# Gate and up projection as seven block products, with the second half of the residual scaling on GpSimd released after the block sums

## The chip, the cores and the metric

One Trainium2 chip, one core. The metric is the device time of one execution, in microseconds, as a median of the runs shown. The engines are TensorE (PE: matmuls; PEld: its weight loads), VectorE (DVE), ScalarE (ACT), GpSimd (POOL) and SyncE (SP), which here issues most DMAs. Each engine works through its own queue in order, and semaphores are the only link between queues.

## What is computed

One encoder layer over 1024 tokens of width 1024, in float32: a layer norm, three mixers (a recurrent one, a 2D neighbourhood attention, a latent attention), an output projection with residual and layer norm, then a gated feed-forward part of inner width 2816 with residual and layer norm. What the change touches is the last part:

```python
        mix = jnp.concatenate([o_rw.astype(h.dtype), o_na.astype(h.dtype), o_mla.astype(h.dtype)], -1) @ w_out[l]
        h = layer_norm(DN_ALPHA * h + mix, ln1_g[l], ln1_b[l])
        ff = (jax.nn.silu(h @ w_ffn_gate[l]) * (h @ w_ffn_up[l])) @ w_ffn_down[l]
        h = layer_norm(DN_ALPHA * h + ff, ln2_g[l], ln2_b[l])
```

## The kernel before

The tokens are 8 row tiles of 128 (or two halves of 512 columns, once turned), the width is 8 slices of 128, the inner width FT = 22 column tiles f of 128. A float32 product is made of three products of rounded operands (type float32r): an operand x is split into hi, its rounded copy, made by ScalarE, and lo = x - hi, made by VectorE; the product is hi\*hi + hi\*lo + lo\*hi.

**Output projection and first norm.** `mix_out` (line 2078) forms a row tile in two PSUM banks with plain float32 matmuls (line 2081). VectorE adds the residual (line 1524), takes the statistics (lines 1488 and 1490), and after four tiles normalises them (line 1498). The normalised tiles are turned by `turn1` (line 2098): 8 slices of 4 transposes each (line 2106), the first half ahead of row tile 6, the second after the first part of gate/up. Even slices are scaled and shifted out of PSUM by ScalarE (`copy_even`, line 1029), odd ones by VectorE (`transposed1`, line 1505); ScalarE rounds each (line 1035) and VectorE makes the remainder (line 1509). From the fifth slice on, a transpose waits until its bank is read. The same norm's row-major output is wanted later as the residual: GpSimd scales each row tile in place with two instructions (lines 781 and 783), four tiles after each turn, and SP writes all 4 MB to DRAM (line 621), since the arena has no room for them.

**Gate and up.** `gate_up` (line 2123) makes one tile f: for gate and up (n), two halves (hf), 8 slices (k) and 3 terms, 96 matmuls of 128x128 by 128x512 (line 2130), into four PSUM banks, the four others being used for the next f. SP loads the raw weight tiles (`gate_up_load`, line 612) when the remainder of the tile before is made; ScalarE makes the rounded copy (`weights_hi`, line 1013), VectorE the remainder (`weights_lo`, line 1512), two tiles ahead. Silu of gate is ScalarE's (line 1048), the product with up is VectorE's (line 1542). Four engines run this as a loop of two tiles; the other stages around it are straight code.

**Down.** The product of the activations with w_down is already made as seven block products in the manner of Strassen and Winograd, in four phases: `RING` (line 58) lists the steps of three phases of 11 steps with two products each (w = 0, 1), 24 matmuls of 128x512 per step (line 2152), and the last product runs alone as phase 3, row tile by row tile. ScalarE (`left_hi`, `right_hi`) and VectorE (`left_lo` line 1551, `right_lo` line 1556) split the operands into a ring of four left and two right slots; VectorE makes block sums of the activations (`sums_of_left`, line 1568) and of w_down (`sums_of_right`, line 1581, `last_of_right`, `difference_of_right`). Between phases it adds the finished products to the residual (`add_product`, line 1604), which SP has brought back. After the third phase VectorE takes the statistics of the last norm (`half_stats`, line 1624), and `centre2` and `scale2` finish six row tiles; two others go to ScalarE and GpSimd (POOL_ROWS = 2).

## Time and profile before

| | |
|---|---|
| median of 3 runs | 1831.33 us (1828.92 to 1832.34) |
| profiled execution | 1832.07 us |
| its span, first to last instruction | 1830.3 us |
| busy: TensorE / VectorE / ScalarE / GpSimd | 92% / 51% / 30% / 20% |
| mean granted clock of TensorE | 0.97 |
| moved over HBM | 93.6 MB, mean 51 GB/s |

"Busy" is the share of the span in which an engine executes; matmuls overlap in TensorE's pipeline, so that the mean length of one is more than the distance between two. The stages that matter lie in the span thus: output projection 975 to 1100, gate and up 1100 to 1598, down products 1598 to 1815, last norm to 1830.

### The profile page before, as it was taken

What the parts mean: (1) busy time and instruction counts of PE and PEld (TensorE: products, weight loads), DVE (VectorE), ACT (ScalarE), POOL (GpSimd) and SP (SyncE); (2) the same over time, 40 slices, a digit from 0 to 9 for tenths busy, and PEclk for the clock granted to TensorE, in tenths of its full rate; (3) what the DMA queues carried; (4) which work ended last, traced back from release to release, by engine and by line L of the source; (5) the groups of instructions that cost most, each with busy time, mean ns of one, the idle gap of its engine ahead of it and who ended that gap; (6) DMA issues with size and microseconds to landing.
All of it is one profiled execution on the core that took longest, in us unless ns stands there. A gap on an engine that the chain in (4) does not pass through costs nothing.

```text
span 1830.3 us, 22866 instructions
## 1 busy us (share of the span) xinstructions
PE 1676.0 (92%) x8984; PEld 1225.0 (67%) x8984; DVE 940.0 (51%) x1327; ACT 552.0 (30%) x1028; POOL 359.6 (20%) x363
## 2 busy tenths in 40 slices
PE   2999987868899997899999997999999999999996
PEld 1788755634556654577774445888888888877885
DVE  7314427866675664667665456211111111299878
ACT  3111147733444332444431012111111111133450
POOL 0800001105600000878870044000000000000002
PEclk9999999988999999899999998999999999999998
DMA  5221000000000000000005001211111111164422
GB/s 199 91 93 46 12 30 1 1 16 1 5 9 4 4 0 15 2 3 2 2 2 218 12 12 69 93 55 59 46 46 46 46 46 46 43 199 159 152 70 92
DMA packets 22703, 93.62 MB, mean 51 GB/s; under 512 B 2576, under 2 KB 4944, under 8 KB 20576
## 3 DMA queue, kind: packets, MB, share of 16 engines
q1 hardware_dynamic: 22160, 87.27, 13.5%
q0 software_dynamic: 464, 5.28, 0.7%
q8 instruction: 52, 0.85, 0.2%
q14 instruction: 27, 0.22, 0.0%
HBM read 79.92 MB, written 12.58 MB: 51 GB/s over the span
## 4 chain that ended last, share of the span: by engine, by line
PE 82%; DVE 11%; ACT 3%; issue 2%; DMA 1%; POOL 0%; SPq 0%; ACTq 0%; DVEq 0%; POOLq 0%
PE psum L2130 26%; PE psum L1724 9%; PE psum L2152 8%; PE psum L2081 6%; PE psum L1882 6%; PE psum L1871 4%; PE psum L1742 2%; PE psum L1850 2%; PE psum L1806 2%; PE psum L1824 1%; PE psum L1787 1%; PE psum L1749 1%; PE psum L1980 1%; PE psum L1976 1%; DVE arena L1283 1%
## 5 line engine op out<-in xcount | busy, mean ns | idle before, releaser
L2130 PE MATMUL psum<-h_hi,w_hi 128*128 128x512 f32 x704 | 275.2, 391 | 11.7 <-DVE h_lo L1509 11.7
L2130 PE MATMUL psum<-h_hi,w_lo 128*128 128x512 f32 x704 | 274.6, 390 | 0.0
L2130 PE MATMUL psum<-h_lo,w_hi 128*128 128x512 f32 x704 | 274.6, 390 | 0.0
L1542 DVE TENSOR_TENSOR arena<-psum,arena 128x1024 f32 (+1 forms) x22 | 27.0, 1225 | 391.2 <-ACT arena L1048 391.2
L2130 PEld LDWEIGHTS psum<-h_hi,w_hi 128*128 128x128 f32 x704 | 132.7, 189 | 39.7 <-DVE h_lo L1509 12.0
L2130 PEld LDWEIGHTS psum<-h_lo,w_hi 128*128 128x128 f32 x704 | 132.7, 188 | 27.8 <-issue 0.2
L2130 PEld LDWEIGHTS psum<-h_hi,w_lo 128*128 128x128 f32 x704 | 132.6, 188 | 27.5
L788 POOL TENSOR_TENSOR arena<-arena 128x1024 f32<-128x1024 f32 x2 | 5.8, 2888 | 655.0 <-ACT arena L1102 655.0
L743 POOL TENSOR_TENSOR arena<-arena,consts 128x512 f32<-128x512 f32 x64 | 80.9, 1285 | 232.0 <-ACT arena L984 231.4
L1882 PE MATMUL psum<-arena 128*128 128x512 f32 x256 | 123.8, 608 | 0.0
L1293 DVE TENSOR_REDUCE stats<-psum 128x1 f32<-128x1024 f32 x64 | 78.0, 1224 | 74.6 <-PE psum L1850 74.0
L2081 PE MATMUL psum<-arena 128*128 128x512 f32 x256 | 112.7, 600 | 1.8 <-DMA arena<-in_w_out 1.8
L2152 PE MATMUL psum<-right_hi,left_hi 128*128 128x512 f32 x264 | 103.5, 392 | 5.3 <-DVE right_lo L1559 5.3
L1724 PE MATMUL psum<-h_hi,w_in_hi 128*128 128x512 f32 x240 | 96.7, 403 | 11.1 <-DVEq L1144 11.1
L1048 ACT ACTIVATE arena<-psum 128x1024 f32 (+1 forms) x22 | 22.6, 1027 | 273.4 <-PE psum L2130 273.3
L2152 PE MATMUL psum<-right_hi,left_lo 128*128 128x512 f32 x264 | 103.5, 392 | 0.0
L2152 PE MATMUL psum<-right_lo,left_hi 128*128 128x512 f32 x264 | 103.4, 392 | 0.0
L1724 PE MATMUL psum<-h_lo,w_in_hi 128*128 128x512 f32 x240 | 96.0, 400 | 0.0
L1724 PE MATMUL psum<-h_hi,w_in_lo 128*128 128x512 f32 x240 | 95.1, 396 | 0.0
L945 ACT ACTIVATE arena<-psum 128x1024 f32<-128x1024 f32 x64 | 65.0, 1022 | 91.0 <-PE psum L1871 90.6
L2081 PEld LDWEIGHTS psum<-arena 128*128 128x128 f32 x256 | 48.9, 192 | 64.6 <-issue 60.4
L754 POOL TENSOR_TENSOR arena<-arena,consts 128x512 f32<-128x512 f32 x64 | 79.9, 1269 | 16.7 <-DVE arena L1426 11.6
(286 smaller groups left out, 3118.4 us busy)
## 6 DMA issues: line engine op xcount, KB each, us to landing
arena<-in_w_gate SPq DMA_DIRECT2D x22, 512.0 KB, 3.2
arena<-in_w_up SPq DMA_DIRECT2D x22, 512.0 KB, 4.5
arena<-in_w_down SPq DMA_DIRECT2D x22, 512.0 KB, 3.7
arena<-in_w_down SPq DMA_DIRECT2D x11, 1024.0 KB, 4.8
arena<-in_w_in SPq DMA_DIRECT2D x15, 512.0 KB, 3.6
arena<-in_x SPq DMA_DIRECT2D x8, 512.0 KB, 10.6
resid_spill<-arena POOLq DMA_DIRECT2D x1, 4096.0 KB, 12.9
arena<-in_w_out SPq DMA_DIRECT2D x8, 512.0 KB, 6.4
```

Source lines behind the costliest of these rows:

```text
L743: pool.tensor_tensor(Lev[d][m % 2], Araw[i % 2][d], four_heads(cst((C_LV if d == 0 else C_LVT) + m - 1)), ALU.mult).then_inc(lev_ready, 1)
L754: pool.tensor_tensor(Xt[d].rearrange("p h (k c) -> p h k c", c=32), spread(Xtcs[i % 2][d]), own_block, ALU.mult).then_inc(xt_full, 1)
L945: act.activation(halves(e_ring[kt % NE]), psum[:, 2 * (kt % 2):2 * (kt % 2) + 2, :], ACT.Exp, scale=MLA_SCALE).then_inc(e_ready, 1)
L1293: v.tensor_reduce(g_max[:, b, t:t + 1], psum[:, g_banks, :], AX.XY, ALU.max, negate=True).then_inc(g_max_ready, 1)
L1724: mm = pe.matmul(bank(2 * b + hf), w[:, P * k:P * k + P], x[k][:, cols], start=(k == 0 and n == 0), stop=(k == KT - 1 and n == 2))
L1742: mm = pe.matmul(bank(t), x[k][:, t * P:(t + 1) * P], wv_parts[k // 2][:, HALF * (k % 2):HALF * (k % 2) + HALF], start=(k == 0 and n == 0) ...
L1806: mm = pe.matmul(bank(4 + b, P), na_et[:, b, j * P:(j + 1) * P], vals[:, first // 2 + j, hp * P:(hp + 1) * P], start=(j == 0), stop=(j == 3))
L1871: mm = pe.matmul(bank(2 * (kt % 2) + hf), k_part[b][0:rows, keys_at], q_part[b][0:rows, hf * HALF:(hf + 1) * HALF], start=(n == 0), stop=( ...
L1882: mm = pe.matmul(bank(6 + hf), vh[b][:, kt, :], e_ring[kt % NE][:, hf * HALF:(hf + 1) * HALF], start=(kt == 0), stop=(kt == NT - 1))
L2081: mm = pe.matmul(bank(mixed_bank(t) + hf), mix[:, k, t * P:(t + 1) * P], w_out[k][:, hf * HALF:(hf + 1) * HALF], start=(k == 2), stop=(k = ...
L2130: mm = pe.matmul(bank(4 * b + 2 * n + hf), w[b][n][:, P * k:P * k + P], x[k][:, cols], start=(k == 0 and i == 0), stop=(k == KT - 1 and i ...
L2152: mm = pe.matmul(bank(4 * w + t), x[:, t * P:(t + 1) * P], right_part(p, part), start=(first and n == 0), stop=(last and n == 2), skip_gro ...
```

## The change

Gate and up of one tile become one 2x2 block problem: the weight side has the blocks gate and up, each with its first and its last 512 of the 1024 inner rows; the other side has the same two halves of the width, by two halves of the tokens. Seven block products replace eight. `FF` is the order of the 154 products, written out for each engine; nothing of this stage is a loop any more. A product is 4 slices x 3 terms = 12 matmuls and uses three PSUM banks per tile (x, y, z); a bank is copied by ScalarE, and read again by VectorE, between the products that accumulate in it.

- VectorE makes 8 double-width sums of the turned rows once (`sum5`, `sum6`, `sum7`, `sum4`) with their remainders (`sum_lo`), and four block sums of raw weights per tile (`block_sum`), three adds of PSUM to copies (`add_part`), two multiplications (`times_up`), and every second tile one sum for the down stage (`first_sum`). ScalarE rounds seven weight halves of 128x512 per tile (`part_to_hi`) into a ring of seven slots, copies PSUM three times (`copy_part`) and makes two silus.
- Both engines prepare the first weight halves between the row tiles of the output projection; of this, two block sums and one remainder are placed after row tile 5.
- GpSimd's scaling of row tiles 4 to 7 waits for the last remainder of the turned block sums. SP writes the residual in two halves.
- The activations of the first 12 tiles go to DRAM (`act_spill`), and come back for the first phase of the down product; 10 stay. Two places of tiles lie in `consts`.
- In the down stage the tiles are paired otherwise, one of the four left sums is made ahead, the left sums trail the steps by two, there are three buffers for the wide w_down tiles instead of two, and half of the last statistics are taken earlier.
- The host reorders w_down for the new pairs.

```diff
+FF = [(0, 1), (0, 2), (1, 1), (1, 2)] + [(f, p) for p in (3, 5, 6, 7, 4) for f in range(2)]
+FF += [(2, p) for p in (1, 5, 2, 6, 3, 7)]
+FF += [(f - (p == 4), p) for f in range(3, FT) for p in (1, 4, 5, 2, 6, 3, 7)] + [(FT - 1, 4)]
...
+            for f in range(2, FT):
+                sp.wait_ge(part_lo, FF_AT[f - 2, 7])
+                sp.dma_start(raw_gate[f % 2], a["w_gate"][f]).then_inc(weights_in[f % 2], 16)
+                sp.wait_ge(part_lo, FF_AT[f - 2, 4])
+                sp.dma_start(raw_up[f % 2], a["w_up"][f]).then_inc(weights_in[2 + f % 2], 16)
+                if f == 4:
+                    put_residual(1)
+                if f % 2 == 0 and 0 <= f - 4 < BACK:
+                    if f > 4:
+                        sp.wait_ge(act_out, 16 * (f - 4))
+                    put_out(f - 4)
+                    put_out(f - 3)
...
             for t in range(NT):
                 pool.wait_ge(ln_tr, 2 * KT + 8 * (t // 4 + 1))
+                if t == 4:
+                    pool.wait_ge(h_lo_ready, 2 * KT + OPERAND_AT[4])
                 own.add(pool.tensor_tensor(resid[:, t, :], resid[:, t, :], ln1_rows[0], ALU.mult))
...
```

VectorE's queue from the second turn on (the steady block last):

```diff
+            turned(1, 5)
+            turned(1, 7)
+            for i in range(2):
+                sum5(i)
+            for i in range(2):
+                sum_lo(5, i)
+            for i in range(2):
+                sum6(i)
+            part_to_lo(0, 7)
+            for i in range(2):
+                sum_lo(6, i)
+            for f in range(2):
+                add_part(f, 0)
...
+            part_to_lo(0, 4)
+            for i in range(2):
+                sum_lo(4, i)
+            for f in range(2):
+                add_part(f, 1)
+            part_to_lo(1, 4)
+            own.wait()
+            for f in range(2):
+                add_part(f, 2)
+            block_sum(2, 0)
+            part_to_lo(2, 1)
+            block_sum(2, 1)
+            for f in range(2):
+                times_up(f, 1)
+            part_to_lo(2, 5)
+            part_to_lo(2, 2)
+            block_sum(2, 2)
+            for f in range(2):
+                times_up(f, 0)
+            part_to_lo(2, 6)
+            part_to_lo(2, 3)
+            block_sum(2, 3)
+            part_to_lo(2, 7)
+            first_sum(1)
...
+            for f in range(2, FT):
+                last = f == FT - 1
+                if not last:
+                    block_sum(f + 1, 0)
+                    part_to_lo(f + 1, 1)
+                if f > 2:
+                    times_up(f - 1, 0)
+                part_to_lo(f, 4)
...
+                    block_sum(f + 1, 1)
+                    part_to_lo(f + 1, 5)
+                add_part(f, 0)
...
```

TensorE's product and its waits, and the changed order of additions and left sums between the phases on VectorE:

```diff
+            def ff_product(f, p):
+
+                x, y, z = (4 * (f % 2) + i for i in range(3))
+                if p == 1 and f >= 2:
+                    pe.wait_ge(ff_ready, count_at(2, f - 2, 1))
...
+                elif p == 6:
+                    pe.wait_ge(part_copied, count_at(3, f, 0))
+                elif p == 7:
+                    pe.wait_ge(part_copied, count_at(3, f, 2))
+                elif p == 4:
+                    pe.wait_ge(part_added, count_at(3, f, 2))
+                if f == 0:
+                    pe.wait_ge(h_lo_ready, 2 * KT + OPERAND_AT[p])
...
+                for i, (w, h) in enumerate(((hi, h_hi_p), (hi, h_lo_p), (lo, h_hi_p))):
+                    if i == 2:
+                        pe.wait_ge(part_lo, FF_AT[f, p])
+                    for k in range(4):
+                        mm = pe.matmul(bank({2: z, 3: y, 5: y}.get(p, x)), w[:, P * k:P * k + P],
+                                       h[k // 2][:, HALF * (k % 2):HALF * (k % 2) + HALF],
+                                       start=(fresh and i == 0 and k == 0), stop=(i == 2 and k == 3), skip_group_check=True)
+                mm.then_inc(ff_done, 1)
...
+            sums_of_left(HF - 2)
+            sums_of_right(0)
+            step_lo((1, 0))
+            sums_of_right(1)
             v.wait_ge(resid2_in, 16 * NT)
...
+            for w in range(2):
+                add_products(0, w)
             for f in range(HF):
-                step_lo((1, f))
+                if f:
+                    step_lo((1, f))
                 if f == 0:
-                    add_products(0)
+                    sums_of_left(HF - 1)
                 last_of_right(f)
-                if f + 1 < HF:
-                    sums_of_right(f + 1)
+                if f + 2 < HF:
+                    sums_of_right(f + 2)
```

## Rows read from the trace of the kernel before

**Rows 1.** The page: busy times, the chain by engine and line, costliest group

```profile
PE 1676.0 (92%) x8984; PEld 1225.0 (67%) x8984; DVE 940.0 (51%) x1327; ACT 552.0 (30%) x1028; POOL 359.6 (20%) x363
...
PE 82%; DVE 11%; ACT 3%; issue 2%; DMA 1%; POOL 0%; SPq 0%; ACTq 0%; DVEq 0%; POOLq 0%
PE psum L2130 26%; PE psum L1724 9%; PE psum L2152 8%; PE psum L2081 6%; PE psum L1882 6%; PE psum L1871 4%; PE psum L1742 2%; PE psum L1850 2%; PE psum L1806 2%; PE psum L1824 1%; PE psum L1787 1%; PE psum L1749 1%; PE psum L1980 1%; PE psum L1976 1%; DVE arena L1283 1%
...
L2130 PE MATMUL psum<-h_hi,w_hi 128*128 128x512 f32 x704 | 275.2, 391 | 11.7 <-DVE h_lo L1509 11.7
```

**Rows 2.** Windows: stretch, length, busy by engine (count), granted clock, DMA share, GB/s

```profile
1150.00:1600.00 450.00, 450.00 (x1987) 372.74 (x1986) 71.12 (x63) 68.48 (x71) 0.00 (x0) 1.00 0.14 47
...
984.00:990.00 6.00, 6.00 (x16) 2.65 (x15) 4.49 (x3) 2.11 (x2) 0.00 (x0) 1.00 1.01 437
...
1072.00:1080.00 8.00, 8.00 (x18) 3.52 (x17) 8.00 (x5) 1.73 (x3) 7.84 (x4) 0.89 0.00 0
...
1128.00:1130.00 2.00, 2.00 (x6) 1.52 (x6) 2.00 (x1) 0.00 (x0) 1.92 (x2) 0.50 0.00 0
...
1606.00:1608.00 2.00, 2.00 (x7) 1.58 (x6) 1.97 (x4) 0.00 (x0) 0.00 (x0) 0.56 0.90 209
```

**Rows 3.** The chain in order of time: start, length, what ran

```profile
1110.59 0.45 PE psum L2106 x4
...
1117.31 4.78 DVE h_lo L1509 x2
...
1122.81 4.80 DVE h_lo L1509 x2
...
1127.65 470.06 PE psum L2130 x2064
```

**Rows 4.** TensorE's waits from 900 us on: total, times, longest

```profile
PE psum L2130 <- DVE h_lo L1509: 11.7, 1, 11.7
PE psum L2152 <- DVE right_lo L1559: 5.3, 3, 2.2
PE psum L2106 <- DVE arena L1505: 3.9, 3, 1.6
```

**Rows 5.** Groups from 1000 us on, as in the page's fifth part

```profile
L1554 DVE TENSOR_TENSOR left_lo<-arena,left_hi 128x512 fp32r<-128x512 f32 x66 | 44.5, 688 | 11.8 <-ACT left_hi L1070 11.7
...
L1070 ACT ACTIVATE left_hi<-arena 128x512 fp32r<-128x512 f32 x66 | 41.2, 630 | 82.8 <-PE psum L2152 81.9
...
L1559 DVE TENSOR_TENSOR right_lo<-arena,right_hi 128x1024 fp32r<-128x1024 f32 x33 | 40.4, 1224 | 5.9 <-ACT right_hi L1083 5.9
...
L1048 ACT ACT_TABLE_LOAD x7 | 9.0, 1283 | 128.5 <-PE psum L2130 128.5
```

**Rows 6.** DMA issues from 930 us on: median us from issue to landing

```profile
arena<-in_w_up SPq DMA_DIRECT2D x22, 512.0 KB, 4.5
...
arena<-resid_spill SPq DMA_DIRECT2D x1, 4096.0 KB, 18.2
```

**Rows 7.** Timeline of VectorE and GpSimd in the second turn

```profile
1115.11 1.48 DVE L1509 TENSOR_TENSOR h_lo<-arena,h_hi 128x512 fp32r<-128x512 f32 x2
...
1117.22 4.86 DVE L1509 TENSOR_TENSOR h_lo<-arena,h_hi 128x512 fp32r<-128x512 f32 x2
1122.01 0.80 DVE L1505 TENSOR_SCALAR arena<-psum,par 128x512 f32<-128x512 f32 x1
...
1127.52 6.71 DVE L1514 TENSOR_TENSOR w_lo<-arena,w_hi 128x1024 fp32r<-128x1024 f32 x2
...
1118.87 2.67 POOL L783 TENSOR_TENSOR arena<-arena 128x1024 f32<-128x1024 f32 x1
```

**Rows 8.** Timeline of TensorE: first matmul after each of the two longer stops

```profile
1605.16 0.47 PE L2152 MATMUL psum<-right_hi,left_hi 128*128 128x512 f32 x1 [2.01 <-DVE right_lo L1559]
...
1669.11 0.47 PE L2152 MATMUL psum<-right_hi,left_hi 128*128 128x512 f32 x1 [2.23 <-DVE right_lo L1559]
```

**Rows 9.** Timeline of VectorE in the last norm: one half statistic of sixteen

```profile
1807.41 0.68 DVE L1625 BATCH_NORM_STATS2 stats<-arena 128x6 f32<-128x512 f32 x1
```

More of the change, by code:

```diff
@@ L64, with count_at, first_of @@
 NSLOTS = 4
+TURN_BANKS = (3, 7, 1, 5)
 POOL_ROWS = 2
+FF = [(0, 1), (0, 2), (1, 1), (1, 2)] + [(f, p) for p in (3, 5, 6, 7, 4) for f in range(2)]
+FF += [(2, p) for p in (1, 5, 2, 6, 3, 7)]
+FF += [(f - (p == 4), p) for f in range(3, FT) for p in (1, 4, 5, 2, 6, 3, 7)] + [(FT - 1, 4)]
+FF_AT = {p: n + 1 for n, p in enumerate(FF)}
+NPARTS = 7
+OPERAND_AT = {1: 4, 2: 8, 3: 12, 5: 14, 6: 16, 7: 18, 4: 20}
+KEPT = 10
+BACK = FT - KEPT
+def count_at(each, f, n):
+    return 2 * n + f + 1 if f < 2 else each * f + n + 1
+def first_of(step):
+    return BACK + 2 * step if step < KEPT // 2 else 2 * step - KEPT
 NDR, NDC = 15, 31
@@ L369, in mixed_bank @@
+        h_part = {p: [[rounded(f"h{p}_{part}{i}", 1024 * at[i], 1024) for i in range(2)] for part, at in
+                      zip(("hi", "lo"), H_PLACES[p])] for p in H_PLACES}
+        T_SUMS = {5: b_first[1], 6: b_second[1], 7: b_first[0], 4: b_second[0]}
+        summand = reg(1024 * 43, 1024).rearrange("p (b c) -> p b c", b=2)
         def mixed_bank(t):
             return 0 if t == 2 else 4 + 2 * (t % 2)
-        w_hi = [[rounded(f"w_hi{b}{n}", *tiles(40 + 4 * b + 2 * n, 1)) for n in range(2)] for b in range(2)]
@@ L374, in hybrid_encoder @@
-        w_lo = [[rounded(f"w_lo{b}{n}", *tiles(41 + 4 * b + 2 * n, 1)) for n in range(2)] for b in range(2)]
-        EARLY = 14
-        def act_tile(f):
-            return reg(1024 * (f + 8 if f < EARLY else f - EARLY), 1024)
-        def act_at(f, hf):
-            return 1024 * (f + 8 if f < EARLY else f - EARLY) + HALF * hf
-        def act_half(f, hf):
-            return reg(act_at(f, hf), HALF)
-        wd_one = [reg(1024 * n, 1024) for n in (22, 23)]
-        wd_both = [reg(1024 * n, 2048).rearrange("p (d f c) -> p d f c", d=2, f=2) for n in (38, 22)]
@@ new lines, in silu @@
+            def silu(f, n):
+                act.wait_ge(part_added, count_at(3, f, n))
+                act.activation(act_half(f, n), act_half(f, n), ACT.Silu).then_inc(silu_ready, 1)
+            for f, p in FF[0:4]:
+                part_to_hi(f, p)
+            sd1(0)
+            for f, p in FF[4:7]:
+                part_to_hi(f, p)
+            turned(0, 0)
+            for n in range(KT):
+                turned_hi(0, n)
+                if n % 2 == 0 and n + 2 < KT:
+                    turned(0, n + 2)
@@ L1090, in step_hi @@
                 right_hi(step)
-            silu(act_tile(FT - 2), 0, 0, FT - 2)
-            step_hi(STEPS[0])
-            silu(act_tile(FT - 1), 1, 0, FT - 1)
-            for step in STEPS[1:]:
+            for f in range(2, FT):
+                last = f == FT - 1
+                copy_part(f, 0)
+                if not last:
+                    part_to_hi(f + 1, 1)
+                part_to_hi(f, 4)
+                copy_part(f, 1)
+                if last:
+                    step_hi(STEPS[0])
+                else:
+                    part_to_hi(f + 1, 5)
+                    part_to_hi(f + 1, 2)
+                silu(f, 0)
+                copy_part(f, 2)
+                if last:
+                    step_hi(STEPS[1])
+                else:
+                    part_to_hi(f + 1, 6)
+                    part_to_hi(f + 1, 3)
+                silu(f, 1)
+                if not last:
+                    part_to_hi(f + 1, 7)
+            for step in STEPS[2:]:
                 step_hi(step)
@@ L1532, in _ @@
                     normalise1(hf)
[L1533 to L1549 removed]
+            for f, p in FF[7:10]:
+                part_to_lo(f, p)
```

640 lines of the change are left out of this document (438 added, 202 removed).

## The prediction

> **What bounds the kernel now.** I read the page first: its busy row and its chain. TensorE is busy for 92% of the span and carries 82% of the chain, and the largest line on it is 2130, the gate and up projections [rows 1]. So a change in the number of matmuls there is worth what a matmul costs there. The windows say what that is: 1,987 matmuls in 450 us at a granted clock of 1.00, 0.2265 us from start to start, with VectorE busy for 71 us and ScalarE for 68 [rows 2]. The 390 ns that the page gives for one matmul [rows 1] is its length in the pipeline, not its cost.
>
> The chain in order of time shows where TensorE stops [rows 3]. Between the turn of the second half of the normalised rows at 1110.59 and the 2,064 back-to-back matmuls that begin at 1127.65, only 32 short transposes run, and 4.78 and 4.80 us go to two pairs of small subtractions on VectorE. The waits of TensorE in the last 930 us are few: 11.7 us there, 3.9 us in the first turn, 5.3 us in the down projection [rows 4]. So this stage and all of the down projection except three stops run at TensorE's pace, and the last 15 us are VectorE's alone.
>
> Timings refer to the profiled execution, 1832.07 us with a span of 1830.3; it is 0.7 us above the median of the three runs, 1831.33. The working calls the start of the second turn T, a product one of the seven (12 matmuls, 2.72 us), f a column tile.
>
> **1. The matmuls.** Before, 2 projections x 2 halves x 8 slices x 3 split terms = 96 per tile, 2,112 in all. After, 7 products x 4 x 3 = 84, 1,848 in all. 264 go, at 0.2265: **-59.8 us**. The row includes everything a matmul costs there, and the new ones have the same shape. The Trainium skill, TensorE: Matmul & The Clock Gate, "Wait — 56ns, not 53.3ns?", gives 215.7 ns start to start for 512 columns at the full clock; the row here is 226.5 ns, and by the page the term would be -56.9.
>
> **2. Does the new steady block stay at TensorE's pace?** One tile is 84 matmuls, 19.0 us. VectorE gets 7 weight remainders, 4 block sums, 3 adds from PSUM, 2 multiplications and half a sum for the down stage: 16.5 operations of 128x512 at 0.69 = 11.4 us (the adds out of PSUM I put at the same). ScalarE gets 7 rounded copies, 3 copies from PSUM and 2 silus, 12 at 0.63 = 7.6 us [rows 5]. Neither is a bound. The tight waits are product 7 on the copy taken after product 6, and product 4 on the add taken after product 7: each has one product, 2.72 us, between, and needs one operation of 0.63 or 0.69 and some 0.2 us of signalling. Weight halves are due six products ahead. I cost the waits at nothing; if the cover went it would be about 1 us a wait. An up tile lands in 4.5 us [rows 6] and is issued five products, some 14 us, before its first use; the gate tile earlier: nothing. The spill of 12 tiles, two per two tiles, goes behind the refill on SP, at a stage that moves 47 GB/s [rows 2]: nothing.
>
> **3. The first turn.** VectorE now makes two block sums and one remainder ahead of its first copy of the turn. Before, that copy followed directly on the statistics, and TensorE waited 3.9 us for it and the next [rows 4]. Three operations at 0.6 delay it: +1.9. The longer stop lengthens the low clock behind it: the eight microseconds after the turn show 0.89 [rows 2]. I take +0.8, between 0 and 2. **+2.7 us**.
>
> **4. The second turn and the first two tiles**, the hard part. The four raw quarters are there at T+6.9, by the rows of before (0.8 us a copy, 0.6 a remainder, no GpSimd yet). From there VectorE works through a chain: 8 sums and 8 remainders of 128x1024 at 1.2 us [rows 5], and 7 operations of 128x512 at 0.66, 23.8 us: T+30.7. I add 1 us for a table load of ScalarE (1.28 us, [rows 5]) and handovers: T+31.7. TensorE has ten products in this stretch (27.2 us) and waits in between.
>
> Then GpSimd is released for rows 4 to 7. The timeline shows what that does [rows 7]. A VectorE operation with both inputs in SBUF waits until the running GpSimd instruction ends: two subtractions that take 1.48 us alone took 4.86, and two of double width 6.71, each ending just behind an instruction of GpSimd. Copies from PSUM (0.80) did not wait. The Trainium skill, SBUF — State Buffer, "Who interferes with whom", says that such an instruction and a GpSimd one that reads SBUF exclude each other, whichever came first; the trace agrees, and this speaks against the new place of GpSimd's work, since VectorE has no slack there either.
>
> GpSimd has 8 instructions of about 2.75 us, 22 us, T+53.7. In VectorE's queue behind the last remainder stand eight operations with two SBUF inputs before tile 0's last multiplication: the remainder of (1,4), sum 0 of tile 2, remainder (2,1), sum 1, the two multiplications of half 1, remainders (2,5) and (2,2). One passes for each GpSimd instruction, T+54.3; then a sum and the multiplication out of PSUM, T+55.7. Product (2,1) waits for that multiplication: it starts at T+56. Without GpSimd, it would start about T+41.
>
> Taking out the ten products leaves 28.8 us, against 17.1 before: **+11.7 us**. The restart behind the stop costs the same half clock in both (0.50, that is 1.2 GHz, in the window at 1128, [rows 2]): nothing. Bounds of this term: -3 (no hold by GpSimd) and +20 (a wait at every handover).
>
> **5. Into the down projection.** Before, the sums of the left blocks stood ahead of the first step, TensorE waited 2.01 us [rows 8] and restarted at a clock of 0.56 [rows 2]. After, the last product 4 and the first two steps are split ahead, and the sums come later. The stop goes (2.0), and the low clock (1.8). Next in line is the multiplication for bank 4, with 2.0 us of matmuls in front of it: enough. **-3.8 us**.
>
> **6. First to second phase.** Before, TensorE waited 2.23 us behind eight additions, one last sum of the right side, two sums, and a step [rows 8]. After, one tile's three left sums (1.9 us) are put behind the eight additions too, and steps still can't run further ahead, since ScalarE fills slots as TensorE frees them. The wait grows to about 4.7 and may bring a low clock of 1 us: **+3.5 us**, between 0 and 5. The second change of phase has the same operations in another order: nothing. DMA: 6 MB of spilled tiles come back during a phase of 60 us with 12.5 MB beside them, 310 GB/s against the 437 that the trace reaches at 984 [rows 2]. Nothing, up to 4 us late.
>
> **7. The end.** Eight half statistics leave the stretch behind the down products; four of them come back inside the last additions. Four remain saved, at 0.60 from start to start [rows 9]: **-2.4 us**. The last product is ready before VectorE asks for it in both kernels, so all of it counts.
>
> The sum: -59.8 + 2.7 + 11.7 - 3.8 + 3.5 - 2.4 = **-48.1**, so 1832.1 - 48.1 = **1784 us**.
>
> **Rivals.** *A. GpSimd's rows hold nothing up.* The operations waited for would be of the kind that pass. Product (2,1) starts at T+41: term 4 falls by 15 and the low clock of the restart (2 us) goes: 1767. For it: TensorE has two products of tile 0 and 1 in that time. Against: rows 7, and the queue as counted. 0.14.
>
> *B. Small stops in the steady block.* The one-product covers are thinner than I think, for instance because a remainder ahead of the add on VectorE waits for ScalarE. 0.5 to 1 us in 20 tiles, 10 to 20 us: about 1799. Against: 5 to 7 us of slack on both engines per tile. 0.18.
>
> *C. The up tile comes late* and the result is **slower than before**. SP issues it only after product 4's remainder, one queue in order with spills. It has some 14 us. It would have to land 16.6 us after its issue for the 20 tiles to lose the 48 us (2.4 each); at the 18.2 us that the big reload of 4 MB needed [rows 6], each of 19 tiles loses 4.2, 80 us: 1864. Against: 4.5 us measured, on a nearly empty queue. 0.03.
>
> *D. The release doesn't do what it says*: GpSimd's rows are short of overlap because VectorE's operations get in first, and GpSimd is the one that is delayed. Then its work spreads to T+60 and VectorE's ends near T+48: 1776, inside the range. 0.05.
>
> **Chances.** The forecast as worked out 0.58, A 0.14, B 0.18, C 0.03, D 0.05, anything else 0.02. Range 1766 to 1801: it takes A and B in, with the bounds of terms 3, 4 and 6 around the forecast, and leaves C and the rest out. No change (within 0.2%, about what a measurement of this kernel can tell) would need 45 us of stops: 0.01. Slower 0.03, faster 0.96.
>
> **What would show it.** Right: 1,848 matmuls of this kind; 0.2265 us each and no wait from tile 3 on; a stop of over 10 us ahead of (2,1), released by a VectorE multiplication out of PSUM; during it, VectorE operations with two SBUF inputs of 2 to 3 us beside GpSimd's rows; no stop at the first step of the down projection; one of 4 to 5 us at the second step of the second phase. Wrong: waits that return in every tile (B), waits for gate or up loads (C), or (2,1) at T+41 (A).

## The result and the profile after

| | before | after |
|---|---|---|
| median of 4 runs each, same chip | 1831.07 us (1828.92 to 1832.34) | 1780.11 us (1779.13 to 1782.65) |
| after / before, 95% interval | | 0.9725 [0.9708, 0.9742] |
| profiled execution / span | 1832.07 / 1830.3 us | 1779.13 / 1777.3 us |
| busy: TensorE / VectorE / ScalarE / GpSimd | 92 / 51 / 30 / 20% | 91 / 63 / 36 / 20% |

The medians are 51.0 us apart, the profiled spans 53.0. "Profiled execution" is the one run of each kernel that left a trace. The profiled execution of after is its fastest run, 1.0 us under the median.

The page of after, beside [rows 1] (its last line beside [rows 6]):

```profile
PE 1617.0 (91%) x8720; PEld 1177.7 (66%) x8720; DVE 1115.0 (63%) x1627; ACT 642.3 (36%) x1224; POOL 357.6 (20%) x363
...
PE 80%; DVE 12%; ACT 3%; issue 2%; DMA 1%; POOL 1%; SPq 0%; DVEq 0%; ACTq 0%; POOLq 0%
...
L1746 DVE TENSOR_TENSOR part_lo<-arena,part_hi 128x512 fp32r<-128x512 f32 x154 | 113.2, 739 | 87.1 <-ACT part_hi L1118 87.1
...
arena<-in_w_up SPq DMA_DIRECT2D x22, 512.0 KB, 3.5
```

There are 264 fewer matmuls and 300 more VectorE instructions. The 154 remainders took 739 ns on average, though most take 0.69: a few of them were held, and the timeline will show which. An up tile lands 3.5 us after its issue, against 4.5 in [rows 6].

TensorE's waits from 900 us on (total, times, longest), beside [rows 4]:

```profile
PE psum L2539 <- DVE arena L1799: 11.6, 1, 11.6
PE psum L2556 <- DVE right_lo L1903: 5.7, 2, 4.7
PE psum L2490 <- DVE arena L1696: 4.4, 2, 3.3
PE psum L2539 <- DVE arena L1782: 4.2, 1, 4.2
PE psum L2539 <- DVE arena L1696: 3.2, 1, 3.2
```

Line 2539 is the product's matmul, 1799 the multiplication by up out of PSUM, 1782 the adds out of PSUM, 1903 the right remainder of the down stage. The 11.6 us stand ahead of product (2,1), as forecast. The windows, beside [rows 2] (stretch, length, busy by engine and count, granted clock, DMA share, GB/s):

```profile
1200.00:1540.00 340.00, 340.00 (x1502) 281.53 (x1501) 192.93 (x290) 128.61 (x216) 0.00 (x0) 1.00 0.22 72
...
1614.00:1616.00 2.00, 0.03 (x1) 0.06 (x1) 2.00 (x4) 0.64 (x1) 0.00 (x0) 0.50 0.90 377
1616.00:1618.00 2.00, 2.00 (x5) 1.61 (x6) 1.34 (x3) 0.00 (x0) 0.00 (x0) 0.50 0.49 115
1618.00:1620.00 2.00, 2.00 (x7) 1.52 (x6) 2.00 (x4) 0.00 (x0) 0.00 (x0) 0.50 0.88 348
```

In the steady block a matmul starts every 340 / 1502 = 0.2264 us at a clock of 1.00, as before the change, with VectorE busy for 57% of it. Behind the stop at the second phase of the down products the clock is 0.50, that is 1.2 GHz. The chain in order of time, beside [rows 3] (start, length, what ran; line 2464 is the output projection):

```profile
983.17 77.27 PE psum L2464 x180
...
1069.18 28.41 PE psum L2464 x64
1097.59 10.90 PE psum L2539 x48
...
1163.54 379.75 PE psum L2539 x1668
```

What held the multiplication is seen on VectorE and on GpSimd, beside [rows 7]. VectorE:

```profile
1145.43 2.85 DVE L1746 TENSOR_TENSOR part_lo<-arena,part_hi 128x512 fp32r<-128x512 f32 x1
1148.39 2.69 DVE L1758 TENSOR_TENSOR arena<-arena 128x512 f32<-128x512 f32 x1
1151.00 5.59 DVE L1796 TENSOR_TENSOR arena<-arena 128x512 f32<-128x512 f32 x2
1156.52 5.57 DVE L1746 TENSOR_TENSOR part_lo<-arena,part_hi 128x512 fp32r<-128x512 f32 x2
1162.19 0.69 DVE L1762 TENSOR_TENSOR arena<-arena 128x512 f32<-128x512 f32 x1
1162.80 1.28 DVE L1799 TENSOR_TENSOR arena<-psum,arena 128x512 f32<-128x512 f32 x2
```

GpSimd, the first and the last of its eight instructions:

```profile
1139.85 2.35 POOL L874 TENSOR_TENSOR arena<-arena,consts 128x1024 f32<-128x1024 f32 x1 [49.99 <-DVE h_lo L1738]
...
1158.87 2.67 POOL L876 TENSOR_TENSOR arena<-arena,consts 128x1024 f32<-128x1024 f32 x1
```

While GpSimd runs, operations that need 0.69 us alone take 2.7 to 2.9; the next behind its last instruction (1161.54) takes 0.69 again. T, the start of the second turn, is 1108.48 here (1097.59 + 10.90), so GpSimd starts at T+31.4 and ends at T+53.1, and (2,1) starts at T+55.1. TensorE, its first matmul behind three stops, beside [rows 8]:

```profile
1143.40 2.08 PE L2539 MATMUL psum<-h_hi,part_hi 128*128 128x512 f32 x4 [4.23 <-DVE arena L1782]
1163.54 2.07 PE L2539 MATMUL psum<-h_hi,part_hi 128*128 128x512 f32 x4 [11.60 <-DVE arena L1799]
1615.97 0.77 PE L2556 MATMUL psum<-right_hi,left_hi 128*128 128x512 f32 x1 [4.65 <-DVE right_lo L1903]
```

### The profile page after: what moved, and what is told of

Read it like the earlier page. It is cut to its first block, busy times and chain, and to the rows that moved or that the text cites. A ratio compares the mean times of both kernels' runs of the same rounds, so it can differ in the third digit from the quotient of the medians.

```text
span 1777.3 us, 23088 instructions
## 1 busy us (share of the span) xinstructions
PE 1617.0 (91%) x8720; PEld 1177.7 (66%) x8720; DVE 1115.0 (63%) x1627; ACT 642.3 (36%) x1224; POOL 357.6 (20%) x363
## 4 chain that ended last, share of the span: by engine, by line
PE 80%; DVE 12%; ACT 3%; issue 2%; DMA 1%; POOL 1%; SPq 0%; DVEq 0%; ACTq 0%; POOLq 0%
PE psum L2539 23%; PE psum L2107 9%; PE psum L2556 9%; PE psum L2464 6%; PE psum L2265 6%; PE psum L2254 5%; PE psum L2125 2%; PE psum L2233 2%; PE psum L2189 2%; PE psum L2207 1%; PE psum L2170 1%; PE psum L2132 1%; PE psum L2363 1%; PE psum L2359 1%; DVE arena L1473 1%
## 5 line engine op out<-in xcount | busy, mean ns | idle before, releaser
L2539 PE MATMUL psum<-h_hi,part_hi 128*128 128x512 f32 x616 | 168.4, 396 | 19.1 <-DVE arena L1799 11.6
L1746 DVE TENSOR_TENSOR part_lo<-arena,part_hi 128x512 fp32r<-128x512 f32 x154 | 113.2, 739 | 87.1 <-ACT part_hi L1118 87.1
L2539 PE MATMUL psum<-h_lo,part_hi 128*128 128x512 f32 x616 | 166.9, 393 | 0.0
L2539 PE MATMUL psum<-h_hi,part_lo 128*128 128x512 f32 x616 | 165.6, 391 | 0.0
L1118 ACT ACTIVATE part_hi<-arena 128x512 fp32r<-128x512 f32 x154 | 96.1, 627 | 148.1 <-PE psum L2539 119.3
L2539 PEld LDWEIGHTS psum<-h_hi,part_hi 128*128 128x128 f32 x616 | 117.1, 191 | 45.2 <-DVE arena L1799 12.0
L2539 PEld LDWEIGHTS psum<-h_lo,part_hi 128*128 128x128 f32 x616 | 117.3, 190 | 24.8
L2539 PEld LDWEIGHTS psum<-h_hi,part_lo 128*128 128x128 f32 x616 | 116.4, 189 | 24.4
```

What stands on the lines that cost most here:

```text
L1118: act.activation(part_ring[(FF_AT[f, p] - 1) % NPARTS][0], raw[:, at:at + HALF], ACT.Copy).then_inc(part_hi, 1)
L1746: v.tensor_tensor(lo, raw[:, at:at + HALF], hi, ALU.subtract).then_inc(part_lo, 1)
L2539: mm = pe.matmul(bank({2: z, 3: y, 5: y}.get(p, x)), w[:, P * k:P * k + P], h[k // 2][:, HALF * (k % 2):HALF * (k % 2) + HALF], start=(fre ...
```

## The experiments

All are edits of after, except one of before. Two kinds of number are given. The median is that of unprofiled and profiled runs together. The experiments ran on three chips, each time beside before, whose median there was 1830.4 to 1831.2 us; the ratio is to that before. The stage lengths come from the one profiled execution of each kernel and are taken from T, because the unchanged code ahead took differing times (see the last section). G is where the chain in order of time reaches the down products, the end is the end of the span:

| kernel | T | T to G | G to end | T to end | median, us | ratio [95% interval] |
|---|---|---|---|---|---|---|
| before | 1110.59 | 487.1 | 232.6 | 719.7 | 1831.07 | 1 |
| after | 1108.48 | 434.8 | 234.0 | 668.8 | 1780.11 | 0.9725 [0.9708, 0.9742] |
| pool_old | 1111.53 | 432.8 | 233.5 | 666.3 | 1778.99 | 0.9717 [0.9701, 0.9733] |
| pool_late | 1116.34 | 429.9 | 233.6 | 663.5 | 1779.83 | 0.972 [0.9704, 0.9736] |
| mult_first | 1110.89 | 429.7 | 234.9 | 664.6 | 1777.05 | 0.9704 [0.9688, 0.972] |
| pool_spread | 1112.71 | 419.8 | 234.7 | 654.5 | 1768.87 | 0.9658 [0.9642, 0.9674] |
| no_rows | 1108.02 | 419.0 | 233.5 | 652.5 | 1762.31 (one run) | |
| before_held | 1110.18 | 481.2 | 232.5 | 713.7 | 1824.63 | 0.9963 [0.9948, 0.9979] |
| turn_early | 1107.71 | 436.3 | 233.3 | 669.6 | 1778.02 | 0.971 [0.9694, 0.9726] |
| left_later | 1111.55 | 434.8 | 231.4 | 666.2 | 1779.47 | 0.9722 [0.9705, 0.9738] |
| seven_more | 1111.34 | 434.8 | 234.0 | 668.9 | 1782.61 | 0.9738 [0.9722, 0.9754] |
| three_edits | 1108.75 | 419.8 | 231.7 | 651.5 | 1762.57 | 0.9626 [0.9604, 0.9647] |
| four_edits | 1108.93 | 419.8 | 226.7 | 646.5 | 1757.88 | 0.9602 [0.9582, 0.9622] |

One execution is a weak measure of a small difference. In the seven edits of after that leave its down stage alone, G to end is 233.3 to 234.9 us, and after and seven_more, which stop at the same places, agree to 0.1 us from T on, while turn_early is 1.5 us longer from T to G with the same stops in the second turn. Differences below some 2 us in one of these columns are therefore not read as effects, unless a stop of TensorE in the trace changed by that much.

### Where GpSimd's rows 4 to 7 run

**pool_old**: released by the turn alone, as in before.

```diff
-                if t == 4:
-                    pool.wait_ge(h_lo_ready, 2 * KT + OPERAND_AT[4])
```

> The changed kernel (1780.1 us) without the wait of GpSimd for the last turned remainder: rows 4 to 7 are scaled from about T+5 on, as in the kernel before. My theory (one VectorE operation with two SBUF inputs per GpSimd instruction, wherever the eight instructions stand): eight operations of the turned sums are held instead of eight behind them, 16 us more in the chain up to the last remainder, and 13 us plus 2 us of low clock less after it; product (2,1) starts at T+57 to T+58 instead of T+55.1, 1782 to 1784 us. Rival 1 (in the old place the hold is covered, so the new place only costs): 1767. Rival 2 (the release is a large part of the gain): over 1792.

The hold moved into the turn and the chain of turned sums. Eight operations of VectorE are held there, one per GpSimd instruction, and six of them are double-wide. One of GpSimd's eight instructions:

```profile
1126.47 3.38 POOL L872 TENSOR_TENSOR arena<-arena,consts 128x1024 f32<-128x1024 f32 x1
```

TensorE from its last stop of this stretch on, ahead of product (0,4), to the first matmuls of (2,1):

```profile
1158.88 1.68 PE L2537 MATMUL psum<-h_hi,part_hi 128*128 128x512 f32 x4 [2.96 <-DVE arena L1780]
...
1166.07 1.07 PE L2537 MATMUL psum<-h_hi,part_hi 128*128 128x512 f32 x4
```

(0,4) began at T+47.4 instead of the T+34.9 of after, but (2,1) stood right behind the pair, at T+54.5, without a stop of its own: GpSimd was done, and the multiplications were worked off in the shadow of (0,4) and (1,4). That is 3 us before the T+57 to T+58 expected, and the median of 1779.0 lies below the 1782 to 1784 expected. The last turned remainder came 13.7 us later than in after (T+44.9 against T+31.2), not 16: held operations fell together with waits for ScalarE that VectorE has there anyway (1.5 and 0.3 us in after). Behind it 14.2 us were saved, not 13. T to end is 2.5 us shorter than in after: (2,1) comes 0.5 earlier, its 1,668 matmuls take 378.2 us instead of 379.75, since they don't begin at half clock (at 0.2264 each they would take 377.6), and 0.5 lies behind G, where nothing was changed. So on the median the new release condition gains nothing by itself, against the old one.

**pool_late**: released two tiles later, with the last weight remainder of tile 2.

```diff
                 if t == 4:
-                    pool.wait_ge(h_lo_ready, 2 * KT + OPERAND_AT[4])
+                    pool.wait_ge(part_lo, FF_AT[2, 7])
```

> The changed kernel with rows 4 to 7 released only after the last weight remainder of tile 2 (product 7). My theory: product (2,1) starts at about T+42 instead of T+55.1 and without the long low clock, 14.5 us less there; but in the 22 us of GpSimd's work VectorE passes 8 operations with two SBUF inputs where the steady block wants 14, so that the adds out of PSUM queued behind them come late and TensorE stops in tiles 3 and 4, 5 to 10 us in all: 1771 to 1776 us. Rival (the steady block has room for it): 1766 with no stops. Rival (the hold is not what delays (2,1)): 1780.

(0,4) began at T+32.0 and (2,1) at T+39.2 with no stop ahead of it, as expected, and two stops came in its place, in the first steady tiles. TensorE:

```profile
1176.19 2.08 PE L2539 MATMUL psum<-h_hi,part_hi 128*128 128x512 f32 x4 [6.90 <-ACT arena L1174]
...
1185.31 1.47 PE L2539 MATMUL psum<-h_hi,part_hi 128*128 128x512 f32 x4 [1.95 <-DVE arena L1782]
```

Their sum, 8.9 us, lies within the 5 to 10 expected. From T to the end it is 5.4 us shorter than after, but the median did not follow: 1779.8 against 1780.1, where 1771 to 1776 were expected. Its profiled execution reached T 7.9 us later than that of after; whether its other runs did too, no run shows. So the four rows in one block cost time at each of the three places tried; by how much less here is not settled.

**mult_first**: the place of the rows kept, the multiplications put ahead of three operations on which tile 2 does not wait yet.

```diff
             part_to_lo(2, 1)
-            block_sum(2, 1)
             for f in range(2):
                 times_up(f, 1)
+            for f in range(2):
+                times_up(f, 0)
             part_to_lo(2, 5)
             part_to_lo(2, 2)
+            block_sum(2, 1)
             block_sum(2, 2)
-            for f in range(2):
-                times_up(f, 0)
```

> The changed kernel with VectorE's queue reordered: the four multiplications of tiles 0 and 1 stand ahead of the weight remainders (2,5) and (2,2) and of block sums 1 and 2 of tile 2. Five instead of eight held operations stand between the adds and the multiplication that product (2,1) waits for. My theory: (2,1) starts three GpSimd instructions, 8 us, earlier, T+47; the operations moved behind it pass in time or stop TensorE for 1 to 2 us: 1772 to 1774 us. Rival (the stop is due to something else than the queue): 1780.

TensorE shows the stop shrunk from 11.60 to 2.55 us, and the next one behind it:

```profile
1156.93 1.19 PE L2539 MATMUL psum<-h_hi,part_hi 128*128 128x512 f32 x4 [2.55 <-DVE arena L1799]
...
1168.82 2.03 PE L2539 MATMUL psum<-h_hi,part_hi 128*128 128x512 f32 x4 [3.44 <-ACT arena L1166]
```

(2,1) started at T+46.0, against T+47 expected: the queue in front of a multiplication did set the stop, at one held operation per GpSimd instruction. But the operations that it overtook were held in turn: ScalarE's next rounding waited for block sum 1 of tile 2, which took 2.88 us beside GpSimd, and the copy that TensorE wanted stood behind it. The net is 4.2 us from T on, a little over half of what I had put, and 3.1 on the medians (1777.05 where 1772 to 1774 were expected); the intervals of the ratios overlap.

**pool_spread**: one row per tile, in tiles 2 to 5, with SP writing each row out by itself.

```diff
-                if t == 4:
-                    pool.wait_ge(h_lo_ready, 2 * KT + OPERAND_AT[4])
+                if t >= 4:
+                    pool.wait_ge(part_lo, FF_AT[t - 2, 7])
...
-                if f == 4:
-                    put_residual(1)
+                if 4 <= f < 8:
+                    put_row(f)
...
-                        act.wait_ge(spilled1, 32)
+                        act.wait_ge(spilled1, 16 * (min(f, 7) - 2))
```

> The changed kernel with GpSimd's rows 4 to 7 spread over the steady block: row t is released after the last weight remainder of tile t-2 and written to DRAM by itself. Runs are compared from the start T of the second turn to the end of the span, since the unchanged stages ahead of T differ by up to 8 us between executions: the changed kernel has 668.8 us there, with all four rows after tile 2 663.5. My theory: 5.5 us of GpSimd in a tile hold two operations, 4 us more for VectorE in a tile of 19 us of which it uses 11, so no stop in tiles 3 to 8 and none ahead of (2,1): 652 to 655 us from T on, 1764 to 1767 in all. Rival (the held operation is always ahead of an add that TensorE waits for): each row costs 2 to 3 us, 660 to 665 from T on, 1772 to 1777 in all.

T to end is 654.5 us, inside the expected 652 to 655; the median, 1768.87, is 1.9 us above the expected 1764 to 1767. It is the only one of the four placements whose interval lies clear below that of after. Its waits of TensorE from 1120 to 1530 us:

```profile
PE psum L2544 <- DVE arena L1701: 3.2, 1, 3.2
PE psum L2544 <- DVE arena L1787: 3.0, 1, 3.0
PE psum L2544 <- ACT arena L1179: 0.4, 1, 0.4
```

The 11.6 us are gone; 3.2 and 3.0 are the stops of the turn and of the turned sums, in which GpSimd has no part (no_rows has the 3.0 too). The hold itself is not: two VectorE operations beside the third of the four rows take 2.9 us each.

```profile
1192.42 2.89 DVE L1759 TENSOR_TENSOR arena<-arena 128x512 f32<-128x512 f32 x1
1195.23 2.88 DVE L1751 TENSOR_TENSOR part_lo<-arena,part_hi 128x512 fp32r<-128x512 f32 x1
```

Two held operations lose 4.4 us there (beside the second and fourth row the two took 1.6 and 2.2 us), and the steady tile has more than that to spare on VectorE: it is 19.0 us long, with 10.8 of work in the window of after (57%). From 1172 us on TensorE has no wait in this stage, so it does not see them.

**no_rows**: leaves out the scaling and shifting of residual rows 4 to 7; GpSimd only signals.

```diff
+                if t >= 4:
+                    pool.memset(resid[0:1, t, 0:1], 0.0).then_inc(resid_ready, 1)
+                    continue
```

> The changed kernel without the scaling of residual rows 4 to 7 on GpSimd (left out: the residual of these rows goes on unscaled and unshifted, one element of each overwritten). It bounds what the hold is worth in all. My theory: no operation of VectorE is held in the stretch behind the second turn, (2,1) starts at T+39.5 as in the kernels with a late release, and T to the end is that of the spread release, 654.5 us, to within 1 us. Rival (the spread release still pays for its rows somewhere): 650 or less.

There is one run, 1762.31 us, with 652.5 from T to end. That is 2.0 under pool_spread, where agreement within 1 was expected, and not the 650 or less of the rival. The whole hold is worth 668.8 - 652.5 = 16.3 us by this trace, and moving the rows to where VectorE has time wins back 14.3 of them. Up to G alone it is 15.8 and 15.0; the remaining 1.2 us between the two kernels lie behind G, where the two do the same work, and are within the scatter of that column. Its TensorE, at the first matmuls of (0,4) and (2,1):

```profile
1141.65 1.71 PE L2542 MATMUL psum<-h_hi,part_hi 128*128 128x512 f32 x4 [2.97 <-DVE arena L1785]
...
1148.80 1.07 PE L2542 MATMUL psum<-h_hi,part_hi 128*128 128x512 f32 x4
```

(2,1) starts at T+40.8, not at the T+39.5 expected here; term 4 had put T+41 for a kernel without GpSimd's rows.

**before_held**: the counter-test in the kernel before. GpSimd's rows 4 to 7 wait for the last remainder of the second turn, so that the four small subtractions run alone.

```diff
+                if t == 4:
+                    pool.wait_ge(h_lo_ready, 2 * KT + 2 * KT)
```

> The kernel before (1831.1 us) with one edit: GpSimd's rows 4 to 7 wait until all 16 remainders of the turned rows are made. Four of the subtractions there are no longer held (2.4 us to 0.6 each, 7 to 8 us in all), the 17.1 us between the second turn and the long row of matmuls become about 9.5; the two remainders of tile 1's weights are held instead, behind 10.9 us of matmuls, at no cost. My theory: 1822 to 1824 us, so a part of what the new release does could be had without block products. Rival (TensorE's stop there is due to the chain ScalarE-VectorE itself): 1831.

VectorE and TensorE, to be read beside [rows 7] and [rows 3]:

```profile
1116.81 1.47 DVE L1511 TENSOR_TENSOR h_lo<-arena,h_hi 128x512 fp32r<-128x512 f32 x2
...
1120.64 6.66 DVE L1516 TENSOR_TENSOR w_lo<-arena,w_hi 128x1024 fp32r<-128x1024 f32 x2 [0.25 <-ACT w_hi L1018]
```

```profile
1120.44 0.80 PE L2132 MATMUL psum<-h_hi,w_hi 128*128 128x512 f32 x1 [4.96 <-DVE h_lo L1511]
```

The pairs fell from 4.86 to 1.47 us, the stop from 11.7 to 4.96, and the products began at T+10.3 instead of T+17.1. 6.0 us fewer from T to end and 5.9 on the medians of the same chip (1824.63 against 1830.54) agree. That is a little less than expected (1822 to 1824), as the stretch fell to 10.3 us and not to 9.5; the interval of the ratio leaves out 1. Now it is the remainders of tile 1's weights that are held (6.66), and nobody waits. So the hold cost time in before as well, and 6 of the 51 us could be had without block products.

### The other terms

**turn_early**: the two block sums and the remainder of term 3 moved from behind row tile 5 to row tile 4.

```diff
                 elif t == 4:
                     part_to_lo(0, 3)
                     part_to_lo(1, 3)
-                elif t == 5:
                     for f in range(2):
                         block_sum(f, 3)
                     part_to_lo(0, 5)
```

> The changed kernel with the two block sums and the remainder that stand between row tiles 5 and 6 moved up behind row tile 4. My theory: VectorE's first copy of the first turn again follows the statistics, TensorE's waits in that turn (4.4 us) go back to 2.6 by the trace of the kernel before (1.6 and 1.0), and the stretch from the start of the 180 matmuls of the output projection to T falls from 125.3 to between 123 and 124: 1778 to 1779 us. Rival (ScalarE sets the turn's pace): 125.3 and 1780.

TensorE's wait in the first turn:

```profile
PE psum L2489 <- DVE arena L1696: 2.6, 2, 1.5
```

The 4.4 us became 2.6, and from the first output-projection matmul to T it took 122.1 us instead of 125.3, more than the 123 to 124 expected, because the low clock behind the turn went too: the 64 matmuls took 27.47 us instead of 28.41. Half of it went again between T and G (436.3 against 434.8): the 1,668 matmuls behind (2,1)'s stop, which was the same, took 381.28 us instead of 379.75. The median, 1778.02, lies within the 1778 to 1779 expected, 2.1 us under that of after, with overlapping intervals.

**left_later**: the three left sums of term 6 moved from the first to the sixth step of the second phase.

```diff
             for f in range(HF):
                 if f:
                     step_lo((1, f))
-                if f == 0:
-                    sums_of_left(HF - 1)
                 last_of_right(f)
+                if f == 5:
+                    sums_of_left(HF - 1)
```

> The changed kernel with the left sums of the last pair moved from behind the eight additions of the first phase to the sixth step of the second phase, where VectorE has room. My theory: TensorE's stop of 4.7 us at the second step of that phase falls by the 1.9 us of the three sums, to 2.8, and the low clock behind it gets shorter or goes: 2 to 4 us less from T to the end (665 to 667 instead of 668.8), 1776 to 1778 in all. Rival (the stop is the w_down load or the ring): 4.7 as before, 1780.

```profile
1617.10 0.76 PE L2556 MATMUL psum<-right_hi,left_hi 128*128 128x512 f32 x1 [2.73 <-DVE right_lo L1903]
```

TensorE's stop went from 4.65 to 2.73, by the three sums' length, as expected, and G to end from 234.0 to 231.4. The stop is 1.9 us of this; that the other 0.7 are clock is not shown, since kernels with the stop of 4.65 differ by more than that among themselves (233.3 to 234.9). The median, 1779.47, is above the 1776 to 1778 expected and cannot be told from that of after.

**seven_more**: one more read-only statistic of 128x512 on VectorE ahead of each weight remainder from tile 3 on, to test the steady block's slack (rival B).

```diff
                 v.wait_ge(part_hi, FF_AT[f, p])
+                if f > 2:
+                    own.wait()
+                    own.add(v.bn_stats(bn[:, 0, 0:6], hi.bitcast(F32)))
                 v.tensor_tensor(lo, raw[:, at:at + HALF], hi, ALU.subtract).then_inc(part_lo, 1)
```

> The changed kernel with one more VectorE operation of 128x512 (a batch-norm statistic of the rounded copy, result unused) ahead of every weight remainder from tile 3 on: seven more per tile, 4.5 to 5 us, 133 operations in all. My theory (TensorE has one product of cover in front of every wait and VectorE 7 us of slack per tile): VectorE is busy for 16 of 19 us and TensorE doesn't stop; 1780 to 1782 us, T to end 669 to 671. Rival (the covers are thin; queue order matters): an add that TensorE waits for comes late once per tile, 0.5 to 2 us in each of 19 tiles, 1790 to 1818 us.

The same window as of after:

```profile
1200.00:1540.00 340.00, 340.00 (x1502) 281.53 (x1501) 267.69 (x416) 127.33 (x214) 0.00 (x0) 1.00 0.21 69
```

There are 126 more operations in it, VectorE is at 79%, and TensorE has the same 1,502 matmuls and the same 434.8 us from T to G. There were no stops in the block, and 4.2 us more of VectorE's work per tile make none. The median, 1782.61, is 0.6 us above the 1780 to 1782 expected and 2.5 above that of after, with overlapping ranges (1782.02 to 1783.48 against 1779.13 to 1782.65); from T on the traces are 0.1 us apart, so that the trace shows no place for those 2.5.

### Together

**three_edits** is pool_spread, turn_early and left_later in one.

> The spread release, the block sums moved out of the first turn and the last left sums moved into the second phase, together. By the three runs alone, from T to the end 668.8 - 14.3 - 2.6 = 651.9 us, and from the output projection's 180 matmuls to T 122.2 instead of 125.3. In all 20 us less than the changed kernel: 1760 to 1763 us. Rival (the edits are worth less together, since the stops share a cause): 1765 to 1768.

It took 651.5 us from T to end, and the median, 1762.57, lies within the 1760 to 1763 expected. TensorE's waits are those of the single edits: 2.6 in the first turn, 3.2 and 3.0 in the second, and 2.7 at the second phase of the down products. From T on, pool_spread and left_later alone would make 668.8 - 14.3 - 2.6 = 651.9. The gain of all three, 17.5 us on the median, is well outside the scatter.

**four_edits** adds `POOL_ROWS = 0`: the last norm's two row tiles that went to ScalarE and GpSimd stay on VectorE.

> As three_edits, and all eight row tiles of the last norm on VectorE instead of two of them on ScalarE and GpSimd. Four operations of VectorE are held by GpSimd there at 3.2 us against 1.2 (8 us); two more row tiles cost VectorE 2.4 us each (4.8): 2.5 to 3.5 us less than three_edits, 1757 to 1760 us. Rival (the held operations are slow for another reason, such as their place behind the statistics): 5 us more than three_edits.

In three_edits, an operation of VectorE in the last norm was held by GpSimd; in four_edits the same kind took 1.28. First three_edits, then four_edits:

```profile
1726.19 0.17 DVE L1982 RECIPROCAL stats<-stats 128x1 f32<-128x1 f32 x1 [1.40 <-ACT stats L1294]
...
1736.50 3.23 DVE L1991 SCALAR_TENSOR_TENSOR arena<-arena,stats 128x1024 f32<-128x1024 f32 x1
```

```profile
1727.15 1.28 DVE L1986 SCALAR_TENSOR_TENSOR arena<-arena,stats 128x1024 f32<-128x1024 f32 x1
```

For row tiles 0 to 3, VectorE made four such operations at 3.2 to 3.4 us beside GpSimd, and now makes eight at 1.28: twice the work in less time. It gained 5.0 us from G to end and 4.7 on the median, more than the 2.5 to 3.5 expected, since the 1.40 us wait for ScalarE's square root, which I had not counted, went too. four_edits is the best version found: 1757.88 us (1757 to 1760 expected), 0.9602 of before, and 22.2 us below after.

## Why the prediction was right

The forecast was 1784 (1766 to 1801); the median is 1780.1. The predicted difference was -48.1, the measured ones are -51.0 (medians) and -53.0 (profiles). Term by term, profile against profile:

| term | forecast | measured | from |
|---|---|---|---|
| ahead of the change, unchanged code | 0 | -3.5 | start of the output projection, 986.7 and 983.2 |
| 3, first turn | +2.7 | +1.4 | output projection to T: 123.9 and 125.3 |
| 1, 2 and 4, gate and up | -48.1 | -49.6 | T to the last product: 487.1 and 437.5 |
| 5 and 6, down products | -0.3 | +0.9 | from there to the last matmul |
| 7, the end | -2.4 | -2.3 | last matmul to end: 15.4 and 13.1 |

(437.5 is the 434.8 of the table with the last product 4, 2.72 us, which runs behind the first down product.)

**Terms 1 and 2** held: 0.2264 us per matmul, and TensorE's waits between 1170 and 1600 us are an empty list. So **rival B** is out, and seven_more shows that the cover was thick. **Rival C** is out as well: no wait of TensorE for gate or up weights appears.

**Term 4** held in mechanism and size: (2,1) at T+55.1 against T+56, GpSimd from T+31.4 to T+53.1 against T+31.7 to T+53.7, one two-input operation per GpSimd instruction. The Trainium skill, SBUF — State Buffer, "Who interferes with whom", says that a VectorE instruction with two SBUF inputs and a GpSimd one that reads SBUF contend, and that the shared ports are an exclusive lock. The trace agrees: such operations took 2.7 to 2.9 us instead of 0.69 until GpSimd was done. Gate and up came out 1.5 us under the forecast: 0.9 of it lie ahead of (2,1), and 0.7 in the restart behind the stop, which cost 2.1 us here and 2.8 in before. **Rival D** is out: the rows did overlap VectorE's operations. **Rival A**, that the rows hold nothing up, is refuted as to this kernel, but its number was nearly right for one in which they don't: 1767 forecast, 1762.3 in no_rows, 1768.9 in pool_spread.

**Term 3** looks too large, 2.7 against a measured 1.4, but the 1.4 rests on a clock in the profile of before that another execution of the same code does not show. The stop did what I said: the output projection resumed 2.1 us later after its start than in before. For "the longer stop lengthens the low clock behind it", +0.8, the profile of before is the odd one. There the 64 matmuls behind the turn took 29.12 us at a clock of 0.80 in the first eight, in after 28.41 at 0.89. But before_held has the same code up to T, and took 27.47 at 1.00 (its row of the chain in order of time, then the window of the first eight microseconds):

```profile
1071.79 27.47 PE psum L2083 x64
```

```profile
1071.79:1079.79 8.00, 8.00 (x20) 3.46 (x20) 8.00 (x6) 2.92 (x5) 7.78 (x3) 1.00 0.00 0
```

All three kernels with the early sums took 27.47 too, and seven of the eight with after's turn 28.36 to 28.50 (pool_late 29.86). So behind the longer stop some 0.9 us more are lost, as far as these executions go. Against before_held the first turn cost 125.3 - 122.2 = 3.1 us, and turn_early took 3.2 back, so the term was sound in size, and the 1.4 of the table is the luck of one profile. Two readings in it were off: of the 3.9 us in [rows 4] only 2.6 lie in the first turn, and the window of 0.89 begins 1.4 us behind the restart.

**Terms 5 and 6** were too small together, -0.3 against +0.9. The stop into the down products went, and the one at the second phase was 4.65 us against 4.7. The step "may bring a low clock of 1 us" was undersized: the matmuls behind it ran at 0.50 from 1616 to 1620, where half the work of 4 us is lost, 2 us. How much it is differs between executions: behind the same stop the first four microseconds show 0.60 in pool_old.

**Term 7** held, -2.3 against -2.4.

The excess of the profiled difference over the sum comes from the code ahead, not from any term: without those 3.5 us it is -49.5 against -48.1. That the sum came so close is in part luck: in this pair of profiles term 3 came out 1.3 under its forecast and terms 5 and 6 1.2 over.

## What to carry to other kernels

GpSimd work off the critical path is not free work: look for VectorE operations with both inputs in SBUF beside it, and cost them at one per GpSimd instruction. Don't ask when the GpSimd work may start but where VectorE has slack, and cut it into pieces that fit there; moving it in one block only moved the stop from one wait to the next. When several edits each gain less than the scatter of whole runs, compare stage lengths from a common point in the trace, add them up, and measure the sum. And look at a second execution of the same code before you read a clock or a microsecond off one trace.

## What the runs showed of the hardware, unexpected

**The hold works both ways.** A GpSimd instruction of 128x1024 took 2.35 us when no VectorE operation with two SBUF inputs was running at its start, even with one held beside it later (the first of the eight in after). It took 2.67 to 2.85 when such an operation of 128x512 had just been let through, and 3.2 to 3.4 behind one of 128x1024.

**The clock behind a short stop is not a matter of the stop's length alone.** It was 0.56 behind 2.01 us [rows 2, 8] and 0.50 behind 2.73 us (left_later, below), but 1.00 in the 4 us behind 2.23 us in before (1669 to 1673) and 1.00 across the 2.55 us in mult_first. In before_held, whose down stage is the same code as in before, the two stops changed places: 1.00 in the 4 us behind the first, 0.64 behind the second. So it is not the place in the code either. What decides was not tried. The windows of left_later, of mult_first and of before_held (two):

```profile
1618.00:1620.00 2.00, 2.00 (x6) 1.52 (x5) 1.76 (x3) 0.00 (x0) 0.00 (x0) 0.50 0.69 164
```

```profile
1156.00:1160.00 4.00, 3.07 (x13) 2.55 (x14) 4.00 (x5) 0.00 (x0) 4.00 (x2) 1.00 0.00 0
```

```profile
1598.84:1602.84 4.00, 4.00 (x18) 3.29 (x19) 3.93 (x7) 1.15 (x2) 0.00 (x0) 1.00 0.72 179
1661.19:1665.19 4.00, 4.00 (x12) 3.15 (x13) 3.38 (x6) 1.06 (x1) 0.00 (x0) 0.64 0.62 221
```

**Identical code ran at different paces at the full clock.** In the input projection, which nothing here touches, 50 us held 216 matmuls in the profile of before and 220 in that of after, both at 1.00. First before, then after:

```profile
100.00:150.00 50.00, 50.00 (x216) 40.22 (x216) 10.91 (x11) 6.18 (x8) 0.00 (x0) 1.00 0.15 47
```

```profile
100.00:150.00 50.00, 50.00 (x220) 40.95 (x219) 11.25 (x12) 6.52 (x9) 0.00 (x0) 1.00 0.14 48
```

In the profiles of before, after and the eleven experiments the output projection began between 982.7 and 989.5 us, with no pattern by edit. The cause is open; it is why the stage lengths are taken from T.
